# The gated mixer's projections in a two-layer mixer kernel: queries of a gate loaded from GpSimd's queue, keys issued ahead of stores, values passed through ScalarE once

## The reference

```
(a_q, a_k, a_v, a_alpha, a_beta, a_gate,
 b_q, b_f_fwd, b_f_bwd, b_i, b_gate, merge) = split_cols(u @ w_in_l)
f_logit = jnp.stack([b_f_fwd, b_f_bwd], axis=2)
f = lb_l + (1.0 - lb_l) * jax.nn.sigmoid(f_logit)
b_g = jnp.log(f).reshape(bsz, length, 2, B_HEADS, B_DK)
b_k = ((1.0 - lb_l) * jax.nn.sigmoid(-f_logit)).reshape(...)
b_q = jax.nn.silu(b_q).reshape(...) * B_DK ** -0.5
...
G = jnp.cumsum(g, axis=-2)      # within a chunk
qg = q * jnp.exp(G)
kd = k * jnp.exp(g_last - G)
```

## Time and profile before

| | |
|---|---|
| median of 3 runs | 4540.08 us (4540.05 to 4543.15) |
| profiled execution: its own time | 4539.8 us |
| its span in the trace | 4538.2 us |
| TensorE matmul busy | 4105.5 us, 90% of the span, 20335 instructions |
| VectorE busy | 1742.0 us, 38% |
| ScalarE busy | 1338.9 us, 30% |
| GpSimd busy | 343.8 us, 8% |
| DMA | 323.01 MB, mean 71 GB/s |

### The profile page before, as it was taken

The page is one execution under the profiler, slowest core; times in us unless marked ns, Lnnn a source line. Parts: engine busy times, 40 slices in busy tenths (PEclk is TensorE's granted clock), DMA queues, the critical chain, the costliest instruction groups (busy, mean ns, idle before and its releaser), DMA issues. The chain is left out here.

```text
span 4538.2 us, 52225 instructions
## 1 busy us (share of the span) xinstructions
PE 4105.5 (90%) x20335; PEld 2175.1 (48%) x20335; DVE 1742.0 (38%) x3175; ACT 1338.9 (30%) x2575; POOL 343.8 (8%) x392
## 2 busy tenths in 40 slices
PE   5899889978679998999999989687999998999998
PEld 2444444434357775444444434332555555555554
DVE  4499624634156665400101025523444442232232
ACT  2233223334245555500000000111555553222211
POOL 0000000000056661000000000000000000000000
PEclk7899999988889999999999999898999999999999
DMA  4122355164755543210101032230000003010110
GB/s 172 42 45 45 62 119 146 60 108 80 116 162 177 181 160 122 79 32 23 47 23 40 15 116 103 74 99 23 3 7 7 6 1 149 28 42 33 37 42 23
DMA packets 576599, 323.01 MB, mean 71 GB/s; under 512 B 417194, under 2 KB 525070, under 8 KB 572431
## 3 DMA queue, kind: packets, MB, share of 16 engines
q1 hardware_dynamic: 569393, 290.41, 23.7%
q0 software_dynamic: 7008, 29.89, 1.7%
HBM read 213.54 MB, written 106.70 MB: 71 GB/s over the span
## 5 line engine op out<-in xcount | busy, mean ns | idle before, releaser
L759 PE MATMUL bank<-uT,gla_inputs_W 128*128 128x512 f32 (+1 forms) x1280 | 520.3, 570 | 69.5 <-DMA gla_inputs_W<-in_w_in 69.5
L1630 PE MATMUL bank<-uT,merge_WG 128*128 128x512 f32 x1024 | 446.5, 595 | 9.6 <-DMA merge_WY<-in_w_b_out 9.6
L759 PEld LDWEIGHTS bank<-uT,gla_inputs_W 128*128 128x128 f32 x1280 | 256.1, 202 | 325.3 <-issue 237.0
L443 PE MATMUL bank<-uT,conv_W 128*128 128x512 f32 (+1 forms) x960 | 376.6, 554 | 2.6 <-DMA conv_W<-in_w_in 2.6
L2475 PE MATMUL bank<-out_W,out_xT 128*128 128x512 f32 x768 | 338.2, 597 | 5.1 <-DMA out_W<-in_w_in 5.1
L1630 PEld LDWEIGHTS bank<-uT,merge_WG 128*128 128x128 f32 x1024 | 195.6, 191 | 255.5 <-issue 245.1
L443 PEld LDWEIGHTS bank<-uT,conv_W 128*128 128x128 f32 x960 | 184.7, 193 | 191.3 <-issue 182.9
L2228 PE MATMUL bank<-kT,attn_qT 96*128 96x512 f32 (+3 forms) x640 | 250.1, 543 | 7.4 <-ACT kT L2285 6.8
L1662 DVE TENSOR_TENSOR merge_row<-bank,merge_sig 128x512 f32<-128x512 f32 x32 | 22.2, 692 | 607.0 <-PE bank L1635 607.0
L1765 PE MATMUL bank<-residual_W,residual_mT 128*128 128x512 f32 x512 | 224.8, 598 | 16.9 <-DMA residual_W<-in_w_out 16.9
L2475 PEld LDWEIGHTS bank<-out_W,out_xT 128*128 128x128 f32 x768 | 145.9, 192 | 182.4 <-issue 182.4
(11 more groups left out here) (370 smaller groups left out, 5572.6 us busy)
## 6 DMA issues: line engine op xcount, KB each, us to landing
scan_dq<-delta_qkv SPq DMA_DIRECT2D x36, 768.0 KB, 4.6
scan_gq<-gla_asks_keys_values SPq DMA_DIRECT2D x36, 768.0 KB, 5.9
gla_asks_keys_values<-gla_inputs_a SPq DMA_DIRECT2D x16, 1152.0 KB, 12.3
delta_qkv<-conv_y SPq DMA_DIRECT2D x12, 1152.0 KB, 9.9
constants_wm<-in_w_mod SPq DMA_DIRECT2D x8, 1536.0 KB, 9.0
gla_inputs_work<-delta_qkv SPq DMA_DIRECT2D x9, 1024.0 KB, 6.1
gla_inputs_q<-gla_queries SPq DMA_DIRECT2D x8, 1152.0 KB, 5.7
gla_asks_keys_values<-gla_inputs_b_ SPq DMA_DIRECT2D x8, 1152.0 KB, 18.9
```

The costliest lines, as they stand in the source:

```text
L443: mm = pe.matmul(bank[:, b, 0:n], W[:, s, k, :], uT[:, k, t0:t0 + n], start=(k == 0), stop=(k == KT - 1))
L759: mm = pe.matmul(bank[:, b, 0:n], W[:, s, k, :], uT[:, k, t0:t0 + n], start=(k == 0), stop=(k == KT - 1))
L1630: mm = pe.matmul(bank[:, q + br, :], WG[:, s, br, k, :], uT[:, k, t], start=(k == 0), stop=(k == KT - 1))
```

## The change

It has three parts, all in `phase_gla_inputs`. The load of a gate's queries into `q`, with its two waits, leaves SyncE's `weights` and becomes a loop at the end of GpSimd's stream; there the first load also waits for the stores of the inverted systems. In SyncE's group spots `keys(n + 1)` is issued ahead of `blocks(n - 1)`. And for value blocks the second pass through ScalarE becomes an empty instruction that raises the same semaphore.

```diff
@@ sync, weights(f)
                 sp.dma_start(W[:, f % 2], w_in[:, col0:col0 + P].rearrange("(k p) n -> p k n", p=P)
                              ).then_inc(w_loaded[f % 2], 16)
-                if kind == "gate":
-                    if n:
-                        sp.wait_ge(D.sem, D.at(n - 1, "q"))
-                    fq = block_of[("query", n % HEADS)]
-                    sp.wait_ge(stored[fq % 2], stored_after[fq])
-                    sp.dma_start(q[:], sq_[n % HEADS]).then_inc(q_loaded, 16)
@@ sync, at a group's spot
                     if n is not None:
                         if n:
-                            blocks(n - 1)
                             if n + 1 < GROUPS:
                                 keys(n + 1)
+                            blocks(n - 1)
@@ gpsimd, behind the stores of the inverted systems
-            pool.wait_ge(x_stored, 16 * (1 + EACH))
+            for n in range(NH2):
+                fq = block_of[("query", n % HEADS)]
+                if n:
+                    pool.wait_ge(D.sem, D.at(n - 1, "q"))
+                else:
+                    pool.wait_ge(x_stored, 16 * (1 + EACH))
+                pool.wait_ge(stored[fq % 2], stored_after[fq])
+                pool.dma_start(q[:], sq_[n % HEADS]).then_inc(q_loaded, 16)
@@ scalar, plain(f, func, between)
-                act.activation(a[:, s, :], a[:, s, :], ACT.Copy, scale=P ** -0.5 if func == ACT.Silu else 1.0
-                               ).then_inc(A("ln"), 1)
+                if func == ACT.Copy:
+                    act.nop(nofuse=True).then_inc(A("ln"), 1)
+                else:
+                    act.activation(a[:, s, :], a[:, s, :], ACT.Copy, scale=P ** -0.5).then_inc(A("ln"), 1)
```

## The result

| | before | changed |
|---|---|---|
| median of 4 runs | 4540.07 us | 4440.89 us (4440.25 to 4441.56) |
| span of the profiled execution | 4538.2 us | 4438.6 us |
| TensorE busy | 4105.5 us, 90% | 4083.5 us, 92% |

The ratio is 0.9785, 95% interval 0.9773 to 0.9797. The forecast was 4441 with 4434 to 4462.

The account below looks back on a forecast made before the run. TensorE's 69.5 us of waits for weights, held on SyncE's queue behind the wait for buffer `q`, were taken as the bound. Queries 90.2, keys 7 and values 2.1 sum to 99.3 us saved, giving 4441 us, range 4434 to 4462.

Parts of the forecast that it names:

- The queries' part: Blocks 8 to 15: without waits for weights they end 90.2 us earlier, 69.5 of waits and 20.7 of slower blocks.
- Room in the steady state: Gates, e being a block's end on TensorE: ScalarE evicts late by 6.5 us, unseen by TensorE; weights land before use.
- e + 40.9: When a gate's two stores have landed: k2 ends at e + 20.9, stores land 19.7 us after issue; ScalarE then evicts.
- The room at the tightest weights: Block 9's weights, behind gate 0's stores: landing near 901.3, needed at 911.3, ten us of room.
- Keys: Group 5's keys issued ahead of group 3's stores: gain 7 us, the middle, with ends 0 and 12.
- 0 to 3.9: TensorE's remaining wait before group 5's products, in us, by whether the stores hold the keys; it was 9.91.
- Values: ScalarE's second pass for values removed: only the last of four passes lacks cover, gain 2.1 us, ends 0 and 2.1.
- Stores as the stall: First rival: late stores hold ScalarE and thereby TensorE; 4486 if half the stalls stay, milder form 4454 to 4467; chance 0.12.
- GpSimd's loads: Third rival: queries' loads on GpSimd's queue set the gates' pace; 4589 at 50 us a load; chance 0.03.
- the ring: VectorE's product q, GpSimd's issue, transfer, next product: pace is load + 2.6, deciding from 28.4 us of load on.
- The order that changes nothing: Fourth rival: SyncE's store waiting for k2 holds the weights as before, only 9 us come, 4531; chance 0.03.
- The trap of descriptor writing: VectorE's 2-port mode blocks GpSimd's DMA descriptors; only gate 0's load can meet two maps, 3 us, sum unchanged.

Follow-up runs that it names:

- e1: Kernel before with only the queries' loads moved to GpSimd's queue, keys and values as before: 4447.73 us, ratio 0.9798.
- e5: Kernel before with two buffers for the queries, their load still on SyncE between weights and stores: 4447.87 us, ratio 0.9796.
- e4: Full change, but queries' loads stay on SyncE, each issued just ahead of the stores of the gate before: 4440.15 us, ratio 0.9783.
- e8: Full change, with group 5's keys also issued ahead of the stores of block 1's values: 4438.5 us.
- e9b: Full change, with block 1's two value stores split, one behind group 3's stores, one behind group 5's: 4435.45 us; changed kernel beside it 4439.73.
- e3: Kernel before with only the values' second pass through ScalarE removed: 4536.43 us, ratio 0.9994.
- e2: Kernel before with only the keys issued ahead of the stores: 4531.9 us, ratio 0.9983.
- e6: Full change, with 8 GpSimd fills of buffer q ahead of each load of gates 1 to 7: 4438.97 us.
- e7: Full change, with 16 GpSimd fills of buffer q ahead of each load of gates 1 to 7: 4528.89 us.

## Why the prediction was right

*The queries' part: 90.2 us forecast.* Measured 482.55 - 391.91 = 90.6, alone (e1) and in the full change. The split into 69.5 of waits and some 20 of slower blocks behind them came as worked out. That the wait and not the load was at fault is shown by e5; that its place and not its queue counted, by e4.

*Room in the steady state.* Here a step was wrong, without price. The prediction had ScalarE start on block f + 2 when the stores of block f land, at e + 40.9, and waiting some 6 us for them. It waits for a gate's stores in none of the gates, and once behind them, at block 15. This is ScalarE at gate 4's first eviction (block 10), then at block 15's:

```profile
952.27 1.28 ACT L858 ACT_TABLE_LOAD   x1
953.57 0.38 ACT L858 ACTIVATE gla_inputs_a<-bank 128x256 f32<-128x256 f32 x1
...
1096.86 0.38 ACT L845 ACTIVATE gla_inputs_a<-bank 128x256 f32<-128x256 f32 x1 [7.03 <-DMA gla_asks_keys_values<-gla_inputs_b_]
```

Block 8 ended near 903.2, so this is e + 50.4, and no idle time stands before it: ScalarE was in the chain of block 9, which I had left out of its own order. Its chain and evictions take 17.4 and 7.7 us of each 30.9. ScalarE, not the stores, has the least room, 6 us a gate. At block 15 no such chain stands between (block 14 is a value), and there the wait of the prediction appears, 7.03 us for gate 7's stores; TensorE does not see it. The room at the tightest weights came as forecast, 11 us for 10: 903.2 - 879.96 = 23.2 us less the 12.0 of their landing. (The sum e + 20.9 + 19.7 is e + 40.6, not 40.9; nothing hangs on it.)

*Keys: 7 us forecast, 0 to 12.* Measured 55.24 - 47.74 = 7.5 in the full change, 6.9 alone. The wait of 2.59 is inside 0 to 3.9. But the 7 had been worked out from group 3's stores, by which group 6 could start at 702.4 to 705.2. It started at 703.09, inside these bounds, because TensorE came then: the step products had been ready by 700.19, sooner than worked out. What held TensorE was the 2.59 us wait and the slower clock behind it, so that the 7 came so close is in part luck. The middle was taken of two opposed effects; e8 and e9b show both are real.

*Values: 2.1 us forecast.* Measured 2.1 at the end of the phase (e3). The changed kernel's own end took 1145.44 - 1119.65 = 25.8 us, 2.5 less than before. The 0.4 over goes with the loads' queue: with the second pass kept, the same stretch took 27.9 us in e1 (loads on GpSimd) and 28.3 in e5 (on SyncE), with it gone 25.8 in the changed kernel and 26.2 in e4 (on SyncE). Why is not shown.

*The rivals.* Stores as the stall: TensorE waits for ScalarE's evictions in no run that is rid of the queries' wait and has no delay added; where that wait was kept, in e2 and e3, one stop of the seven ended with an eviction (10.1 and 10.3 us), so evictions and weights were late by about as much. GpSimd's loads: the ring exists, costs nothing at 26.3 us (e6) and sets the pace at 41.1 (e7), with the forecast bound of 28.4 between them, and had 5.7. The order that changes nothing: refuted by e1. Up to the scans' first load the change saves 1246.59 - 1145.44 = 101.2 us, and the span 99.6; later phases, whose instructions are the same, gave back 1.6, which is within what repeated runs of one kernel differ by.

## What to carry to other kernels

A queue that issues in order turns each wait in it into a wait for all that stands behind. Ask of each wait what it holds up, and put it next to a later wait of the same chain, give the data a second buffer, or use an idle queue: with each of the three TensorE's last stretch here was the same 391.91 us. When one wait goes, list each engine's own order for two rounds of the loop, not only the transfers, to find which has the least room. And a short stop of TensorE cost more than its length here (below).

## What the runs showed of the hardware

*Stops and clock.* Seven stops of 6.7 to 11.4 us cost 21 us more (90.6 - 69.5) in the blocks behind them. The granted clock was 0.84 in the window of one stop and its block, and 1.00 where there was no stop. Even the 2.59 us wait of the changed kernel was followed by 8.78 us for 16 records that take 7.13, at a granted clock of 0.81 from 694 to 703 us.

*GpSimd's fills and VectorE's maps.* In the kernel with 8 fills, VectorE's groups from 868 to 1100 us are:

```profile
L1050 DVE TENSOR_SCALAR gla_inputs_b_<-gla_inputs_b_,lbT 128x2304 f32<-128x2304 f32 x7 | 22.7, 3247 | 0.0
L1068 DVE TENSOR_TENSOR gla_inputs_a<-gla_inputs_a,gla_inputs_q 128x2304 f32<-128x2304 f32 x8 | 20.5, 2558 | 24.6 <-DMA gla_inputs_q<-gla_queries 13.6 <-ACT gla_inputs_a L873 10.9
L1070 DVE TENSOR_TENSOR gla_inputs_b_<-gla_inputs_b_,gla_inputs_lf 128x2304 f32<-128x2304 f32 x8 | 20.4, 2551 | 0.0
```

The map took 3247 ns, in the changed kernel 1413. The product q (L1068) says nothing here, as it comes only after the fills and the load. The product k2 (L1070) does: it starts as the fills start (868.08 and 868.22 us) and took 2551 ns with and without them. So in these runs a fill on GpSimd slows the fast map to more than twice and leaves a product of two tensors alone. The Trainium skill (SBUF — State Buffer, Who interferes with whom) says that VectorE in a 2-port mode and GpSimd exclude each other from a shared port pair for a whole instruction, that a `tensor_scalar` can be in such a mode, and that a `tensor_tensor` has none and contends only with GpSimd's reads, of which a fill has none. The trace agrees.

The trap of descriptor writing, for which the prediction cites the Trainium skill, had one chance in the changed kernel: gate 0's load was issued at 852.74 while two fast maps ran from 851.60 to 854.47. It landed in 5.5 us, the other seven in 5.4 to 5.9. With 8 fills the median was 7.3 us, with 16 it was 5.5, so the fills alone don't lengthen a load; what did was not taken apart.

*Issue time on SyncE.* The second of two stores of 1152 KB in pieces of 128 bytes held its queue for 8.0 to 9.8 us here, and the issue of the weights right behind it took 7 to 8 more. Behind nothing of the kind the weights' issue took 0.4 us.
